# An expert loop on one core: the scatter moves into the next expert's gate/up, and every second weight refill moves to ScalarE's DMA queue

## The reference, cut to what matters

```
logits = rmsnorm(h) @ w_router + b_router          # 32 experts
top_val, top_idx = top_k(logits, 4); gates = softmax(top_val)
for each expert e, for its frames xb with gates g:
    gu   = xb @ w_gate_up[e] + b_gate_up[e]         # 1024 x 2048 weights, 8 MB
    act  = (clip(gu_lin) + 1) * (x_glu * sigmoid(1.702 * x_glu)),  x_glu = min(gu_glu, 7)
    y    = act @ w_down[e] + b_down[e]              # 1024 x 1024 weights, 4 MB
    acc[frames of e] += y * g
out = rmsnorm(h + acc, g_final)
```

## Time and profile before

| what | value |
|---|---|
| median of three runs | 1144.58 us |
| the profiled execution | 1144.32 us, span 1142.2 us |
| PE busy | 1069.9 us, 94% of the span |
| DVE, ACT, POOL busy | 343.9, 197.2, 23.5 us |
| mean granted clock of PE | 0.995 |
| DMA, whole span | 437.93 MB, mean 383 GB/s |
| DMA, slices 10 to 39 of 40 | 425 to 429 GB/s |

### The profile page before, as it was taken

One profiled execution on the slowest core, in us unless ns is written; L12 is line 12 of the kernel. 1 busy time (PEld: TensorE's weight loads), 2 busy tenths in 40 slices (PEclk: granted clock), 3 DMA queues, 4 the chain that ended last, 5 costly groups with the idle time before them and its releaser, 6 DMA issues.

```text
span 1142.2 us, 12824 instructions
## 1 busy us (share of the span) xinstructions
PE 1069.9 (94%) x5419; PEld 486.1 (43%) x5420; DVE 343.9 (30%) x573; ACT 197.2 (17%) x323; POOL 23.5 (2%) x53
## 2 busy tenths in 40 slices
PE   8979999999999999999999999999999999999996
PEld 7978998733333333333333333333333333333332
DVE  8555654422222222222222222222222222222223
ACT  6522644500000000000000000000000000000002
POOL 5200000000000000000000000000000000000000
PEclk9999999999999999999999999999999999999999
DMA  9963565799999999999999999999999999999993
GB/s 352 345 217 131 159 247 221 295 386 427 428 429 426 428 429 426 427 428 427 427 428 427 428 428 427 428 429 426 428 429 428 425 429 428 427 427 428 428 427 155
DMA packets 52006, 437.93 MB, mean 383 GB/s; under 512 B 5184, under 2 KB 23024, under 8 KB 27376
## 3 DMA queue, kind: packets, MB, share of 16 engines
q1 hardware_dynamic: 51856, 437.10, 92.2%
q10 hardware_dynamic: 96, 0.02, 0.0%
HBM read 435.47 MB, written 1.05 MB: 382 GB/s over the span
## 4 chain that ended last, share of the span: by engine, by line
PE 84%; DVE 10%; ACT 5%; issue 1%; DMA 0%; ACTq 0%; DVEq 0%
PE ps L734 39%; PE ps L766 20%; PE ps L476 7%; PE ps L534 6%; PE ps L777 5%; PE ps L750 2%; DVE lin L1330 2%; DVE glu L1333 2%; DVE glu L1326 2%; DVE lin L1327 2%; ACT sig L819 2%; ACT xg_sb L819 2%; PE ps L723 1%; PE ps L499 1%; ACT w_hi L819 1%
## 5 line engine op out<-in xcount | busy, mean ns | idle before, releaser
L734 PE MATMUL ps<-slot,xT 128*64 128x512 f32 x2048 | 444.9, 592 | 0.1
L734 PEld LDWEIGHTS ps<-slot,xT 128*64 128x64 f32 x2048 | 143.2, 137 | 283.9 <-issue 277.2
L766 PE MATMUL ps<-slot,sig 128*64 128x512 f32 x1024 | 226.8, 595 | 8.0 <-ACT sig L819 8.0
L1339 DVE TENSOR_TENSOR h_rows<-ps,h_rows 128x1024 f32<-128x1024 f32 x64 | 75.4, 1220 | 271.4 <-PE ps L777 271.4
L1326 DVE TENSOR_SCALAR glu<-ps 128x512 f32<-128x512 f32 x32 | 22.1, 692 | 370.5 <-PE ps L734 370.5
L766 PEld LDWEIGHTS ps<-slot,sig 128*64 128x64 f32 x1024 | 70.7, 137 | 143.5 <-issue 127.9
L990 ACT ACTIVATE sig<-glu 128x512 f32<-128x512 f32 x32 | 20.1, 629 | 546.7 <-DVE glu L1326 546.7
L1088 DVE TENSOR_TENSOR w_lo<-ring,w_hi 128x1024 fp32r<-128x1024 f32 x56 | 69.3, 1245 | 75.9 <-ACT w_hi L819 75.8
L777 PE MATMUL ps<-xg_sb,g_sb 64*128 64x512 f32 x256 | 63.6, 615 | 22.3 <-ACT xg_sb L819 22.3
L819 ACT ACTIVATE xg_sb<-ps 128x512 f32<-128x512 f32 x65 | 38.8, 597 | 241.7 <-PE ps L766 230.0
L819 ACT ACTIVATE w_hi<-ring 128x1024 fp32r<-128x1024 f32 x56 | 58.8, 1060 | 86.4 <-PE ps L476 55.3
(11 more groups left out here) (190 smaller groups left out, 697.0 us busy)
## 6 DMA issues: line engine op xcount, KB each, us to landing
slot<-in_w_gate_up SPq DMA_DIRECT2D x128, 2048.0 KB, 27.2
slot<-in_w_down SPq DMA_DIRECT2D x64, 2048.0 KB, 26.7
ring<-in_w_in SPq DMA_DIRECT2D x8, 1024.0 KB, 13.8
ring<-in_w_v SPq DMA_DIRECT2D x4, 1024.0 KB, 10.5
ring<-in_w_out SPq DMA_DIRECT2D x4, 1024.0 KB, 12.4
ring<-in_w_k SPq DMA_DIRECT2D x4, 1024.0 KB, 6.3
ring<-in_w_q SPq DMA_DIRECT2D x4, 1024.0 KB, 5.2
ring<-in_w_o SPq DMA_DIRECT2D x4, 1024.0 KB, 5.0
```

The costliest lines, as they stand in the source:

```text
L734: mm = pe.matmul(ps[CAP * half:CAP * (half + 1), bank, :], lhsT, w[:, a * CHUNK + bank * D + half * HALF:a * CHUNK + bank * D + (half + 1) ...
L766: mm = pe.matmul(ps[CAP * half:CAP * (half + 1), bank_y, :], lhsT, w[:, r * D + half * HALF:r * D + (half + 1) * HALF], start=False, stop= ...
L1339: dve.tensor_tensor(h_rows[:, t, :].rearrange("p (a n) -> p a n", a=2), ps[:, b:b + 2, :], h_rows[:, t, :].rearrange("p (a n) -> p a n", a ...
```

## The change: what it does

1. PE: `scatter(s - 1)` is no longer issued after `down(s - 1)` but inside `gate_up(s)`, between the matmuls of its first and second chunk. The scatter of the last expert stays at the end.
2. DVE: `add_back(s - 1)` moves with it, to the front of iteration `s`, ahead of `select(s + 1)`.
3. Refills: SP issues only the even chunks. The odd ones are issued by ScalarE, on its own DMA queue, at three places of its loop: before `sigmoid(s)`, after `tokens_out(s + 1)` and after `y_out(s)`. At each place it first waits until the second of two chunks is used, and then issues the one odd refill that belongs to the pair. ScalarE's loop is unrolled for it, and DVE's loop has its first two iterations outside.

```diff
 for n in range(RING, TOTAL):                    # SP
+    if n % 2:
+        continue
     sp.wait_ge(chunks_used, n - RING + 1)
     sp.dma_start(slots[SLOT_ORDER[n % RING]][:], expert_source(...)).then_inc(big_full[n % RING], 16)

-def gate_up(s, par, wait_chunk, ahead=1):       # PE
+def gate_up(s, par, wait_chunk, ahead=1, between=None):
     ...
         mm.then_inc(chunks_used, 1)
+        if c == 0 and between is not None:
+            between()
 for s in range(E):
-    gate_up(s, s % 2, ring_chunk)
+    def scatter_last(s=s):
+        if s > 0:
+            scatter(s - 1)
+    gate_up(s, s % 2, ring_chunk, between=scatter_last)
     gather(s + 1)
     turn_gates(s, s % 2)
     bias_down(s % 2)
     turn_act(s)
     turn_tokens(s + 1)
     down(s, ring_chunk)
-    scatter(s)
+scatter(E - 1)

-with act_e.Fori(0, E) as s:                     # ScalarE
+def refill(first_used, last_used):
+    act_e.wait_ge(chunks_used, last_used + 1)
+    for n in range(first_used + RING, last_used + 1 + RING):
+        if n % 2 and n < TOTAL:
+            act_e.dma_start(slots[SLOT_ORDER[n % RING]][:], expert_source(...)) \
+                .then_inc(big_full[n % RING], 16)
+for s in range(E):
+    refill(s * PER_EXPERT, s * PER_EXPERT + 1)
     sigmoid(s)
     tokens_out(s + 1)
+    refill(s * PER_EXPERT + 2, s * PER_EXPERT + 3)
     gates_out(s)
     act_out(s)
     y_out(s)
+    refill(s * PER_EXPERT + 4, s * PER_EXPERT + 5)

+def prepare_and_activate(s, par):               # DVE
+    select(s + 1, s + 1, par); weigh(s + 1, s + 1, par); activate(s); tokens_out(s + 1, par)
+prepare_and_activate(0, 1)
+add_back(0)
+prepare_and_activate(1, 0)
-with dve.Fori(0, E // 2) as turn:
+with dve.Fori(1, E // 2) as turn:
     for u in range(2):
-        select, weigh, activate, tokens_out, add_back(s)
+        add_back(e0 + (u - 1))
+        prepare_and_activate(e0 + u, (u + 1) % 2)
+add_back(E - 1)
```

More of the change, by code:

```diff
@@ L1006, in _ @@
             most = load_most(act_e)
-            with act_e.Fori(0, E) as s:
+            def refill(first_used, last_used):
+                act_e.wait_ge(chunks_used, last_used + 1)
+                for n in range(first_used + RING, last_used + 1 + RING):
+                    if n % 2 and n < TOTAL:
+                        act_e.dma_start(slots[SLOT_ORDER[n % RING]][:], expert_source(n // PER_EXPERT, n % PER_EXPERT)) \
+                            .then_inc(big_full[n % RING], 16)
+            for s in range(E):
+                refill(s * PER_EXPERT, s * PER_EXPERT + 1)
                 sigmoid(s)
                 tokens_out(s + 1)
+                refill(s * PER_EXPERT + 2, s * PER_EXPERT + 3)
                 gates_out(s)
@@ L1350, in _ @@
             most = load_most(dve)
-            with dve.Fori(0, E // 2) as turn:
+            def prepare_and_activate(s, par):
+                select(s + 1, s + 1, par)
+                weigh(s + 1, s + 1, par)
+                activate(s)
+                tokens_out(s + 1, par)
+            prepare_and_activate(0, 1)
+            add_back(0)
+            prepare_and_activate(1, 0)
+            with dve.Fori(1, E // 2) as turn:
                 e0 = turn * 2
                 for u in range(2):
[L1354 to L1359, removed]
+                    add_back(e0 + (u - 1))
+                    prepare_and_activate(e0 + u, (u + 1) % 2)
+            add_back(E - 1)
             def again(b, e, k):
```

## The result

| | before | after |
|---|---|---|
| median | 1144.58 us (1143.41 to 1145.04, 4 runs) | 1151.03 us (1149.98 to 1152.78, 4 runs) |
| ratio | | 1.006, 95% interval 1.0042 to 1.0078 |
| profiled execution, span | 1144.32, 1142.2 us | 1149.98, 1148.2 us |

The account below looks back on a forecast made before the run. PE was taken to bind up to the last expert, DMA from there. Chunk 189 landing 3.4 + 4.9 = 8.3 us later, PE's saving hidden, gave 1152.9 us; its own range 1150 to 1156, 8 in 10 for 1145.0 to 1160.0.

Parts of the forecast that it names:

- The reading of the bound: Whole loop before the change: PE binds up to the last expert, DMA from there, with no slack between them.
- The scatter's 21.7 us: PE ahead of each scatter: 31 waits of 0.70 us go, 21.7 us of schedule, worth 0 while transfers' end stays.
- Rival E: PE binds after all, landings not being what it waits for: 1123 to 1127 us; folded into rival C, chance 0.11.
- PE's waits for transfers: PE in the changed loop: waits start near expert 15 or 16 and total about 30 us.
- ScalarE's issues: Three issue places in ScalarE's loop: the one before the gates' copy costs 0 or 4 us; no long issues expected.
- The start, +3.4 us: First refills: chunk 11 goes out only when chunk 1 is used, so the DMA hole grows 3.43 us, delaying all after.
- The order, +4.9 us: End of the stream: chunk 189 lands together with 190 instead of one chunk ahead, costing 4.9 us.
- Rival B: Refills on two queues: engines take turns by whole transfers, landings come singly, only the hole's 3.4 us remain: 1148.0 us; chance 0.12.
- The rate, 0: All refills: sharing two queues leaves the DMA rate unchanged, taken as 0, with ends -5 and +34 us.
- C: All 180 refills: two queues together are faster, -8.9 us per per cent of rate; chance 0.11, 0.08 ending faster.
- D: Refills on two queues: switching between them costs rate, 1158 us at 0.6%, 1187 us at 3.8%; chance 0.15.
- the other odd refills open no hole: Odd refills after 11: issued 3.4 to 6 us after their slot is free, but SP's queue holds work, so no new hole.

Follow-up runs that it names:

- e5: Kernel before with every refill bringing only 7/8 of its bytes, PE's work unchanged: 1144.50 us, ratio 1.0004 to the kernel before.
- e1: Kernel before with only the scatter and add_back moved, all refills on SP in order: 1143.40 us, ratio 0.9984 to the kernel before.
- e6: Changed kernel with every refill bringing only 7/8 of its bytes, PE's work unchanged: 1120.87 us, ratio 0.9804 to the kernel before.
- e2: Kernel before with only the odd refills moved to ScalarE's queue, scatter still after down: 1153.69 us, ratio 1.0067 to the kernel before.
- e3: Changed kernel, but chunk 11, the first refill, issued by SP when chunk 0 is used: 1152.74 us, ratio 1.0072 to the kernel before.
- e9: Kernel before with scatter moved, all refills on SP, refill 11 in four 512 KB parts issued early: 1144.63 us, ratio 1.0002 to the kernel before.
- e11: Kernel before with scatter moved, all refills on SP, refill 11 and chunk 189 each in two halves: 1142.47 us, ratio 0.9984 to the kernel before.
- e8: Changed kernel with parities swapped, SP issuing the odd refills and ScalarE the even ones: 1146.57 us, ratio 1.0014 to the kernel before.

## Why the prediction was right

**The reading of the bound** held at every point. The DMA lead runs out at the end of the kernel before: e5 (nothing from lighter transfers) and e1 (nothing from a shorter PE schedule) show both edges of it.

**The scatter's 21.7 us** of schedule are there (e6: 23.1, with the small gaps around the scatter) and are hidden (e1: 0.1 us). Rival E falls with the waits. PE's waits for transfers were to be about 30 us: chunk 189 is first used 897.5 us after chunk 0 in the changed kernel and 866.3 after it in e6, where no wait in the loop is ended by a transfer: 31.2 us. They were to begin near expert 15 or 16 and begin at expert 15.

**ScalarE's issues** were bounded at 0 to 4 us and taken as 0. Its engine and its queue in order of time, an expert with the issue ahead of the gates' copy and one without:

```profile
1067.94 0.60 ACT L826 ACTIVATE xg_sb<-ps 128x512 f32<-128x512 f32 x1 [0.36 <-PE ps L710]
1067.95 0.34 ACTq L1020 DMA_DIRECT2D slot<-in_w_gate_up  x1
1068.44 0.38 ACT L826 ACTIVATE g_sb<-ps 128x256 f32<-128x256 f32 x1
...
1097.30 0.60 ACT L826 ACTIVATE xg_sb<-ps 128x512 f32<-128x512 f32 x1 [0.36 <-PE ps L710]
1097.79 0.38 ACT L826 ACTIVATE g_sb<-ps 128x256 f32<-128x256 f32 x1
```

The issue passes while the copy runs; the next copy starts 0.50 us after the first with it and 0.49 without. No issue lasted long either: at most 0.37 us on ScalarE's queue and 0.34 on SP's in the loop of the changed kernel.

**The start, +3.4 us.** Busy tenths of the DMA engines, 222 to 262 us in 40 slices, chunk 0 first used at 223.75:

```profile
DMA  2000000008579999999999999999999999999999
```

The hole is eight slices instead of five. Chunk 12 lands at 243.6, 19.9 us after the loop's start, instead of 16.3 us after it (225.91 to 242.1): 3.6 us later.

**The order, +4.9 us.** 189 lands 897.4 us after the loop's start instead of 888.6: +8.8 us in all, 8.3 forecast. Rival B (turns by whole transfers) falls with the pairs 0.2 us apart: the engines take turns inside a chunk.

**The rate, 0.** From chunk 12 (243.6) to 190 (1121.0) the changed kernel moves 178 chunks in 877.4 us, 4.93 us each, as the kernel before. Rivals C and D fall by their own test, the GB/s row. The rule of the Trainium skill ("DMA: Bandwidth & Descriptors", "Issuing engines are not separate DMA queues") that two issuing engines interleave on the same DMA engines and save only issue time agrees with 426 to 429 GB/s on two queues.

**What was off.** The loop lost 8.2 us, as summed (8.3); the timed median lost 6.45. In the profiled execution 2.2 us of the difference lie ahead of the loop; whether they do in the other three is not on record. The median is within the range; e2, with the same loop, lost 8.55 by the medians (1153.69 against 1145.14 on its chip). One sentence of the prediction was right only by chance: that the other odd refills open no hole holds because the first hole is there (e3). And the fixed part of a packet comes out of the prediction's own two figures as (4 x 155.7 - 612.5) / 3 = 3.4 ns, not 3.6; nothing else changes by it.

## What to carry to other kernels

When PE and the DMA are both near full, compare the queue's time from issue to landing at the start and at the end of the loop: if it grows until PE meets a transfer, the next microsecond saved on PE is worth nothing, and what is left is how much of PE's work stands behind the last landing. A later start of the stream is paid in full (3.6 us here); an earlier one brought nothing (e9, e11), since the next refills came no earlier. Cut the last transfer that PE waits for into pieces with their own semaphores rather than speed up the loop. Splitting one saturated, ordered stream over two queues gave no rate and lost the order: transfers issued together landed in pairs, the earlier-needed member late by one transfer, and any wait that one issuer adds delays its share whenever the queue is near empty. If a stream is split all the same, let the queue that is issued without further waits carry the chunks that PE needs first (e8, +2.3 us instead of +8.2; the parts of that gain were not tested singly).

## What the runs showed of the hardware

Two queues with 2 MB transfers share the 16 engines inside a transfer, evenly enough that two transfers issued together land within 0.2 us of each other, 12.8 us after their issue, where one alone takes 7.7, and at an unchanged 427 to 428 GB/s. After an empty queue the engines needed about 2 us to get to full rate (98, 295, 131, 131, then 393 GB/s in half-microsecond slices in e3), so each hole costs more than its width. 512 KB parts of 4 KB a partition ran at some 250 GB/s for their first 6 us in e9, a case that stays open.

An issue of a 2 MB transfer takes 0.33 us on SP's queue with fewer than nine transfers outstanding there. With nine or ten, some last up to 2.8 us in the kernel before and up to 6.7 us in e1 (61 of its 181 refills over 0.5 us). In the kernel before one issue, begun at 1033.47 with nine outstanding, ended 2.81 us later, at the landing of chunk 173. It cost no rate: e1's loop is that of the kernel before. With the refills on two queues no issue of a refill in the changed kernel took more than 0.37 us, with at most four earlier ones outstanding on either.
